# Swiglu block of a four-part float32 model on one core: gate and up products by seven block products, the down product behind all of them, the S5 table steps in new places

## Chip, core and metric

The kernel runs on one core of one Trainium2 chip, in float32 throughout. The metric is the device time of one execution in microseconds; the median of three runs before the change is 1338.49 us (1334.94 to 1342.81).

## What is computed

Two blocks over 256 tokens of width 1024. The first has two layers: a gated delta rule mixer and a swiglu, then an S5 mixer (a diagonal state space model, rewritten as convolution tables) and a mixture of eight swiglu experts. The second has pooling and neighbourhood attention and a squared-relu MLP. The change is in the swiglu of the first layer and in the S5 parameter work that is done beside it:

```python
D_FF = 11 * D_MODEL // 4                       # 2816
def swiglu(x, w1, w3, w2):
    return (jax.nn.silu(x @ w1) * (x @ w3)) @ w2
x = layer_norm(ALPHA * x + h, ln_g[i, 0], ln_b[i, 0])
f = swiglu(x, ffn_w1[j], ffn_w3[j], ffn_w2[j])
x = layer_norm(ALPHA * x + f, ln_g[i, 1], ln_b[i, 1])
```

## The kernel before

The program of each engine is written out by hand, and each engine runs its own in order; they meet at semaphores (`wait_ge`, `then_inc`). PE is TensorE, DVE VectorE, ACT ScalarE, POOL GpSimd, SP the engine whose queue carries nearly all loads; ACT and POOL issue some DMAs too. All tiles lie in one buffer, `arena`, by hand-kept offsets, and eight PSUM banks.

**Swiglu.** The 2816 columns of the hidden layer are 11 chunks of 256 (`FF_CHUNKS`), 22 tiles m of 128. x stands transposed in `xT` (8 k-blocks of 128 by 256 tokens). For a tile, `t_form` multiplies 8 weight blocks of w1 into the left half of bank 4 or 5, then 8 of w3 into the right half, each with 256 columns (the tokens). The chunk 0 is done in token halves (`half_form`), since the second half of x comes later from the layer norm. ACT takes silu of the left half into `hsil`, DVE multiplies it with the right half into `hT`. One chunk later `swiglu_down` adds the chunk's part of the down product into banks 0 to 3: 8 products with 512 columns. A float32 matmul stands as two MATMUL records in the trace. So products of gate and up and the down product alternate, chunk by chunk. SP loads a chunk as three DMAs of 1 MB (w1 and w3 in pieces of 1 KB, w2 in pieces of 4 KB) into three sets of tiles (`FF_SETS`).

**S5 work beside it.** `s5_step(m, half)` puts parameter transposes (`s5_transposes`), the transposes of the table W (`s5_turn`) and the kernel products (`s5_kernel`) between tiles: at m = 3 and 4, `S5_TURN_AT`, `S5_KERNEL_AT`. DVE makes angles, powers and the input table `Bb` behind tiles 3 to 5, and half of table V (`s5_v_table`, part 0) at `S5_TABLE_AT`. POOL waits for `Bb` (`bb_ready`), then makes for each of four pieces the table W (six operations of 1024 elements in a partition), two copies into `Bbd`, and its half of V (four of 1152 elements). Piece j+1 waits for the transposes of piece j (`w_tr`) and for its kernel products (`kd_done`). DVE takes the kernel products from PSUM (`s5_take_kernel`) and adds the skip term with two small operations per half (`s5_skip_blocks`, L1024 and L1027); ACT copies W back (`take_w`) and stores the kernel to DRAM (`store_kernel`). After the swiglu comes a layer norm, whose weights POOL loads when its last table is done, and the product with s5_w_in (L2149).

**The fill.** POOL stores zeros into `k_scratch` (semaphore `kz_stored`). ACT waits for them behind the silu of tile 1 and then issues one DMA that fills `slot_rows` in DRAM with zeros, 9600 KB, which the experts need much later.

**The model to follow.** The MLP of the second block already has seven block products in place of eight (`up_product`, `weight_sums`, L2455 and L1329 to L1334): each product multiplies a block or a sum of blocks of the weights with a block or a sum of blocks of x, and DVE makes the sums.

## Time and profile before

| | |
|---|---|
| median of 3 runs | 1338.49 us |
| the profiled execution: time, span | 1341.43 us, 1339.6 us |
| granted TensorE clock, mean | 0.987 |
| PE busy | 1292.6 us, 96% of the span |
| DVE, ACT, POOL busy | 38%, 16%, 13% |
| chain that ended last | PE 91%, DVE 5%, ACT 2% |

The span reaches from the first to the last instruction. The chain is followed back from the last instruction, at each step to what released it or to the instruction before it on its engine. Where PE has 91% of it, other engines count only where PE waits for them.

### The profile page before, as it was taken

How to read it: one execution, taken by the hardware profiler on the slowest of the kernel's cores; microseconds unless marked ns; L12 is line 12 of the kernel's file. 1: busy time of each engine (PE TensorE's matmuls, PEld its weight loads, DVE VectorE, ACT ScalarE, POOL GpSimd, SP SyncE). 2: the span in 40 equal slices, each digit the busy share in tenths (PEclk: the TensorE clock that was granted, in tenths of full speed). 3: DMA queues.
4: the chain of work that ended last, by engine and by line, in shares of the span. 5: the costliest groups of instructions: out<-in, count | busy, mean ns of one | idle time of the engine just before them, and what ended most of it. 6: DMA issues, size and time to landing. Idle time of an engine off the chain costs nothing.

```text
span 1339.6 us, 24413 instructions
## 1 busy us (share of the span) xinstructions
PE 1292.6 (96%) x10757; PEld 852.5 (64%) x10757; DVE 506.1 (38%) x982; ACT 220.9 (16%) x440; POOL 172.7 (13%) x132
## 2 busy tenths in 40 slices
PE   7998999999999999899999999999999979999997
PEld 6887987777777667645544444444445745999443
DVE  0645543334154545613211101110053164555555
ACT  1462223120111110512010101001011021111000
POOL 1020000306566600000200000000033000000000
PEclk9999999999999999999799999999999999999999
DMA  9434010599535267664899999999999060344530
GB/s 341 144 112 157 2 64 0 152 335 314 172 118 169 67 163 116 168 271 164 358 409 414 408 417 417 410 408 407 411 336 255 13 239 0 126 155 161 189 125 32
DMA packets 96934, 292.01 MB, mean 218 GB/s; under 512 B 5916, under 2 KB 43264, under 8 KB 84576
## 3 DMA queue, kind: packets, MB, share of 16 engines
q1 hardware_dynamic: 82288, 260.46, 53.2%
q0 software_dynamic: 4800, 14.67, 3.7%
q10 hardware_dynamic: 9776, 15.86, 3.6%
q8 instruction: 54, 0.88, 0.3%
q14 instruction: 16, 0.13, 0.0%
HBM read 274.19 MB, written 16.78 MB: 217 GB/s over the span
## 4 chain that ended last, share of the span: by engine, by line
PE 91%; DVE 5%; ACT 2%; issue 1%; DMA 0%; POOL 0%; DVEq 0%; ACTq 0%; POOLq 0%
PE bank L1788 19%; PE bank L2283 17%; PE bank L2300 9%; PE bank L2455 7%; PE bank L2493 7%; PE bank L1801 6%; PE bank L2093 5%; PE bank L2223 4%; PE bank L1760 3%; PE bank L2149 2%; PE bank L1794 2%; PE bank L1921 1%; PE bank L2172 1%; PE bank L1935 1%; PE bank L2109 1%
## 5 line engine op out<-in xcount | busy, mean ns | idle before, releaser
L1788 PE MATMUL bank<-xT,arena 128*128 128x256 f32 x1248 | 278.5, 382 | 2.2 <-ACT arena L1499 1.4
L1788 PEld LDWEIGHTS bank<-xT,arena 128*128 128x128 f32 x1248 | 236.5, 191 | 40.1 <-issue 6.1
L2283 PE MATMUL bank<-arena 128*32 128x352 f32 x3072 | 230.2, 461 | 0.7 <-DVE arena L1164 0.7
L2283 PEld LDWEIGHTS bank<-arena 128*32 128x32 f32 x3072 | 93.8, 111 | 134.4 <-issue 133.1
L2300 PE MATMUL bank<-arena 128*32 128x256 f32 x2112 | 115.4, 379 | 0.0
L2493 PE MATMUL bank<-arena 128*128 128x512 f32 x224 | 96.7, 592 | 0.7 <-DVE arena L1341 0.7
L2300 PEld LDWEIGHTS bank<-arena 128*32 128x32 f32 x2112 | 64.7, 110 | 50.3 <-issue 2.4
L1209 DVE TENSOR_TENSOR arena<-arena,bank 128x352 f32<-128x352 f32 x24 | 19.3, 804 | 204.4 <-PE bank L2283 204.4
L2493 PEld LDWEIGHTS bank<-arena 128*128 128x128 f32 x224 | 42.3, 190 | 53.6 <-issue 49.5
L2093 PE MATMUL bank<-arena 128*128 128x512 f32 x144 | 63.6, 594 | 0.0
L1034 DVE TENSOR_TENSOR arena<-arena,bank 128x256 f32<-128x256 f32 x22 | 9.2, 420 | 135.3 <-ACT arena L1583 135.3
L2455 PE MATMUL bank<-arena 128*128 128x128 f32 x512 | 58.5, 275 | 0.0
L2455 PEld LDWEIGHTS bank<-arena 128*128 128x128 f32 x512 | 57.8, 192 | 0.0
L1801 PE MATMUL bank<-arena 128*128 128x512 f32 x128 | 55.9, 593 | 0.5 <-DVE arena L1299 0.5
L1760 PE MATMUL bank<-const,arena 128*128 128x128 f32 x296 | 43.5, 284 | 11.5 <-DVE arena L1309 5.6
L2223 PE MATMUL bank<-arena 128*128 128x512 f32 x112 | 50.2, 609 | 2.6 <-issue 2.6
L1760 PEld LDWEIGHTS bank<-const,arena 128*128 128x128 f32 x296 | 35.1, 146 | 18.6 <-DVE arena L1309 5.6
L2093 PEld LDWEIGHTS bank<-arena 128*128 128x128 f32 x144 | 26.9, 190 | 30.9 <-issue 30.7
L2455 PE MATMUL bank<-xT,arena 128*128 128x128 f32 x384 | 44.5, 275 | 0.0
L2455 PEld LDWEIGHTS bank<-xT,arena 128*128 128x128 f32 x384 | 43.8, 192 | 1.0 <-issue 1.0
L1801 PEld LDWEIGHTS bank<-arena 128*128 128x128 f32 x128 | 23.9, 190 | 29.2 <-issue 28.2
L2223 PEld LDWEIGHTS bank<-arena 128*128 128x128 f32 x112 | 21.7, 195 | 29.8 <-issue 29.8
(401 smaller groups left out, 1416.3 us busy)
## 6 DMA issues: line engine op xcount, KB each, us to landing
arena<-moe_w SPq DMA_DIRECT2D x64, 1408.0 KB, 13.7
arena<-moe_w SPq DMA_DIRECT2D x24, 1536.0 KB, 15.5
arena<-ffn_w SPq DMA_DIRECT2D x33, 1024.0 KB, 10.2
arena<-gdn_w_in SPq DMA_DIRECT2D x8, 2048.0 KB, 10.9
arena<-w_up SPq DMA_DIRECT2D x8, 2048.0 KB, 9.0
arena<-w_down SPq DMA_DIRECT2D x8, 2048.0 KB, 7.7
slot_rows<-arena ACTq DMA_DIRECT2D x1, 9600.0 KB, 47.4
arena<-s_w_glu SPq DMA_DIRECT2D x4, 2048.0 KB, 11.9
```

Of the source, the lines that this page charges most:

```text
L1209: V_.tensor_tensor(mh[:, t].rearrange("p (x f) -> p f x", x=FE_T), msil[:, t].rearrange("p (f x) -> p f x", x=FE_T), banks[2 * t + 1][:, 0 ...
L1760: return nc.tensor.transpose(dst, src, const[0:k, C_ID, 0:k])
L1788: last = mm(bank[:, at:at + SEQ], w[:, k, P * m:P * m + P], x[:, k, :], start=(k == 0), stop=(k == KT - 1))
L1794: last = mm(bank[:, at + P * n:at + P * n + P], w[:, k, P * m:P * m + P], xT[:, k, P * n:P * n + P], start=(k == 0), stop=(k == KT - 1))
L1801: last = mm(bank, x[:, k0 + k, P * n:P * n + P], w[:, k], start=(k0 + k == 0), stop=(k0 + k == total - 1))
L2093: last = mm(banks[2 * n + hf][:, :], hT[:, c % 2, k, P * n:P * n + P], f2[c % FF_SETS][:, k, 512 * hf:512 * hf + 512], start=(c == 0 and k ...
L2149: last = mm(banks[s // 2][32 * q:32 * q + 32, 256 * (s % 2):256 * (s % 2) + 256], x_sub[:, k, s], w[:, 256 * q:256 * q + 256], start=(k == ...
L2223: last = mm(banks[4 * c + 2 * hf + n][:, :], hidT[:, k, P * n:P * n + P], glu[2 * hf + c][:, k], start=(i == 0), stop=(i == KT - 1))
L2283: last = mm(banks[i][32 * q:32 * q + 32, 0:EW1], xg[:, t, EK * s + kk], w[:, kk, EW1 * q:EW1 * q + EW1], start=(s == 0 and kk == 0), stop= ...
L2300: last = mm(y_bank[t][32 * q:32 * q + 32, 0:EW2], mhT[:, t, 32 * x:32 * x + 32], m2[c][:, x % 3, EW2 * q:EW2 * q + EW2], start=(x == 0), s ...
L2455: last = mm(bank[:, P * m:P * m + P], lhs[:, k, P * m:P * m + P], rhs[:, k], start=(i in (1, 2, 5) and m == k == 0), stop=(k == 3), skip_g ...
L2493: last = mm(d_bank[i][:, :], lhs[:, k], rhs[:, k], start=(d == k == 0), stop=(d == 7 and k == 1))
```

## The change

- Gate and up products of a chunk become seven products of 8 matmuls with 128 columns (`ffn_product`, names "1" to "7"): blocks are halves of k, of the chunk's 256 columns and of the tokens, and w1 and w3 go side by side. "1", "6", "7" and "4" add into one bank, "5" and "3" into another, "2" has its own. The order on PE is 1, 2 of chunks 0 and 1, then for each chunk c: 5(c), 6(c), 4(c-1), 3(c), 7(c), 1(c+1), 2(c+1), but no 1 and 2 behind chunk 0.
- The sums: four on the weights per chunk (`f_sum`, 1024 elements each, DVE; those of chunk 0 on POOL, ahead of the layer norm), four on x once (`f_s1`, ...). `f_sum` "1" of chunk c+1 waits for the load of chunk c+1; sum 4 of chunk c stands behind it.
- ACT copies products 1, 5 and 6 out of PSUM (`f_keep`), DVE adds them (c11, c12, c22), ACT takes silu, DVE multiplies (`f_gate`) into `f_tile`, which holds all 22 tiles.
- Weights of w1 and w3 have two buffers in place of three. Loads for chunk c+2 wait for product 7 and sum 4 of chunk c. The loads of chunk 1 come early, beside those of chunk 0.
- All down products stand behind chunk 10. The w2 loads go into places that come free.
- The S5 pieces of DVE stand behind chunks 2 to 8, `Bb` behind chunk 8; DVE's tables and kernels come after the last chunk, in the order table 0, kernel 0, table 1, kernel 1, table 2, table 3, kernel 2. PE's turns and kernels stand between the down chunks. ACT's stand in one loop behind its last chunk.
- The fill of `slot_rows` stands on ACT behind chunk 0.

```diff
-FF_SETS = 3
-S5_FIRST = 3
-S5_TURN_AT = (9, 13, 16, 19)
-S5_KERNEL_AT = (11, 15, 18)
-S5_TABLE_AT = (7, 10, 13, 16)
+S5_FIRST = 2
+S5_TURN_AT = (0, 3, 7)
+S5_KERNEL_AT = (2, 5)
...
+            def gate_loads(c):
+                cols = slice(FC * P * c, FC * P * (c + 1))
+                if c >= 2:
+                    sp.wait_ge(product, nth_p["7", c - 2])
+                    sp.wait_ge(first_sums, 4) if c == 2 else sp.wait_ge(t_sums, nth_t["4", c - 2])
+                load(sp, ("ffn_w1", c), 4 + c % 2, f13[c % 2][:, 0], w1[:, :, cols])
+                load(sp, ("ffn_w3", c), 4 + c % 2, f13[c % 2][:, 1], w3[:, :, cols])
...
-            out_load(0)
-            swiglu_loads(0)
+            gate_loads(0)
+            gate_loads(1)
             sp.wait_ge(kq_done, 4)
             sp.wait_ge(q_used, 1)
             out_load(1)
             sp.wait_ge(lv_p, 24)
             out_load(2)
             out_load(3)
-            sp.wait_ge(y_done, 4)
-            for c in range(1, FF_CHUNKS):
-                swiglu_loads(c)
+            sp.wait_ge(in_tile, 28)
+            out_load(0)
+            for c in range(2, FF_CHUNKS):
+                gate_loads(c)
...
+            sp.wait_ge(product, nth_p["7", last_c - 1])
+            sp.wait_ge(t_sums, nth_t["4", last_c - 1])
+            down_load(0)
+            down_load(1)
+            sp.wait_ge(product, nth_p["7", last_c])
+            sp.wait_ge(t_sums, nth_t["4", last_c])
+            down_load(2)
+            down_load(3)
+            sp.wait_ge(product, nth_p["4", last_c])
+            sp.wait_ge(mlp_v, nth_v["c22", "f", last_c])
+            down_load(4)
+            down_load(5)
+            for c in (6, 7, 8, 9, 10):
+                sp.wait_ge(down_done, (1, 2, 4, 5, 6)[c - 6])
+                down_load(c)
+                if c == 8:
+                    load(sp, ("s5_in", 0), 7, s5_in_w[0], rows(A["s5_w_in"][0], 0, 4))
+            sp.wait_ge(down_done, 8)
+            load(sp, ("s5_in", 1), 8, s5_in_w[1], rows(A["s5_w_in"][0], 4, 4))
             sp.wait_ge(kz_stored, 64)
             sp.wait_ge(xrow_loaded, 16)
+            table_loads(0)
             sp.wait_ge(down_done, FF_CHUNKS - 2)
+            table_loads(1)
+            sp.wait_ge(y_done, 8)
+            table_loads(2)
...
+            arrived(pool, ("ffn_w3", 0))
+            pool.wait_ge(in_tile, 32)
+            b11, b12, b21, b22 = f_blocks(0)
+            nc.gpsimd.tensor_tensor(f_t1, b12, b11, ALU.subtract).then_inc(first_sums, 1)
...
+                if c == S5_FIRST:
                     s5_angles()
+                    s5_multiples(range(0, 5))
+                elif c == S5_FIRST + 1:
+                    s5_multiples(range(5, 9))
+                    s5_reduced()
+                elif c == S5_FIRST + 2:
                     s5_take_c(1)
+                elif c == S5_FIRST + 4:
                     s5_powers()
+                elif c == S5_FIRST + 5:
+                    s5_ratio()
+                elif c == S5_FIRST + 6:
                     dve.wait_ge(s5_read, 3)
                     s5_input_table()
...
+            V_.tensor_tensor(f_s1, a21, a22, ALU.add).then_inc(s_sums, 1)
...
+            def f_sum(i, c):
+                b11, b12, b21, b22 = f_blocks(c)
+                if i == "1":
+                    arrived(dve, ("ffn_w3", c))
+                    dve.wait_ge(product, nth_p["5", c - 1])
+                    dve.wait_ge(first_sums, 4) if c == 1 else dve.wait_ge(t_sums, nth_t["2", c - 1])
+                    ins = V_.tensor_tensor(f_t1, b12, b11, ALU.subtract)
+                elif i == "2":
+                    dve.wait_ge(product, nth_p["6", c - 1])
+                    dve.wait_ge(t_sums, nth_t["1", c] if c == 1 else nth_t["4", c - 1])
+                    ins = V_.tensor_tensor(f_t2, b22, f_t1, ALU.subtract)
+                elif i == "3":
+                    dve.wait_ge(t_sums, nth_t["1", c])
+                    ins = V_.tensor_tensor(b12, b22, b12, ALU.subtract)
+                else:
+                    dve.wait_ge(product, nth_p["4", c - 1])
+                    dve.wait_ge(t_sums, nth_t["2", c])
+                    ins = V_.tensor_tensor(f_t4, b21, f_t2, ALU.subtract)
+                ins.then_inc(t_sums, 1)
...
+                V_.tensor_tensor(f_cb[:, :, 0], pair(banks[2 + c % 2]), f_u2, ALU.add).then_inc(mlp_v, 1)
+                dve.wait_ge(product, nth_p["7", c])
+                V_.tensor_tensor(f_cb[:, :, 1], pair(banks[c % 2]), f_p5, ALU.add).then_inc(mlp_v, 1)
...
+            f_first(0)
+            for c in range(FF_CHUNKS):
+                if c < last_c:
+                    f_sum("1", c + 1)
+                if c:
+                    f_sum("4", c)
+                if c < last_c:
+                    f_sum("2", c + 1)
+                if c:
+                    f_gate(c - 1, False)
+                f_gate(c, True)
+                if c < last_c:
+                    f_sum("3", c + 1)
+                f_others(c)
+                s5_pieces(c)
+                if c < last_c:
+                    f_first(c + 1)
+            f_gate(last_c, False)
+            for j, take in ((0, 0), (1, 1), (2, None), (3, 2)):
                 for q in range(2):
+                    p0 = PIECE * j + 4 * q
+                    s5_v_table(V_, link, slice(p0, p0 + 4), 0, t_v).then_inc(v_ready, 1)
+                    dve.wait_ge(v_ready, 2 * j + q + 1)
+                if take is not None:
+                    s5_take_kernel(take)
+                    s5_skip_blocks(take, 0)
+                    s5_skip_blocks(take, 1)
...
+            for c in range(FF_CHUNKS):
+                f_keep("5", c, banks[2 + c % 2], f_p5, "p5", ("c22", "f", c - 1) if c else None)
+                f_keep("6", c, banks[c % 2], f_u2, "u2", ("c12", "f", c - 1) if c else None)
+                if c:
+                    f_silu_others(c - 1)
+                f_silu_first(c)
+                if c < last_c:
+                    f_keep("1", c + 1, banks[(c + 1) % 2], f_p1, "p1", ("c11", "f", c))
+                if c == S5_FIRST - 2:
                     act.wait_ge(kz_stored, 64)
...
+            f_silu_others(last_c)
+            for j in range(NPIECE):
+                take_w(j, 0)
+                take_w(j, 1)
+                if j < NPIECE - 1:
+                    store_kernel(j)
...
+                if i == "1":
+                    arrived(pe, ("ffn_w3", c))
+                    if c >= 2:
+                        pe.wait_ge(mlp_a, nth_a["c21", "f", c - 2])
+                    lhs, rhs = b11, a11
+                elif i == "2":
+                    if c >= 2:
+                        pe.wait_ge(mlp_v, nth_v["c11", "f", c - 2])
+                    lhs, rhs = b21, a12
+                elif i == "5":
+                    if c >= 2:
+                        pe.wait_ge(mlp_v, nth_v["c12", "f", c - 2])
+                    summed(1)
+                    pe.wait_ge(s_sums, 1)
+                    lhs, rhs = f_t1, f_s1
+                elif i == "6":
+                    pe.wait_ge(mlp_a, nth_a["p1", "f", c])
+                    summed(2)
+                    pe.wait_ge(s_sums, 2)
+                    lhs, rhs = f_t2, f_s2
+                elif i == "3":
+                    pe.wait_ge(mlp_a, nth_a["p5", "f", c])
+                    pe.wait_ge(s_sums, 4)
+                    lhs, rhs = b22, f_s4
+                elif i == "7":
+                    pe.wait_ge(mlp_a, nth_a["u2", "f", c])
+                    summed(3)
+                    lhs, rhs = b12, a21
+                else:
+                    pe.wait_ge(mlp_v, nth_v["c22", "f", c])
+                    summed(4)
+                    lhs, rhs = f_t4, a22
+                for w in range(2):
+                    for k in range(4):
+                        last = mm(bank[:, P * w:P * w + P], lhs[:, w, k], rhs[:, k], start=(i in ("1", "2", "5") and w == k == 0),
+                                  stop=(k == 3), skip_group_check=True)
+                last.then_inc(product, 1)
...
+            ffn_product("1", 0)
+            ffn_product("2", 0)
+            ffn_product("1", 1)
+            turn_x(xres, 1, 0)
+            ffn_product("2", 1)
+            need_x()
+            for c in range(FF_CHUNKS):
+                ffn_product("5", c)
+                ffn_product("6", c)
+                if c:
+                    ffn_product("4", c - 1)
+                if c == S5_FIRST:
+                    s5_transposes(0)
+                ffn_product("3", c)
+                ffn_product("7", c)
+                if c == S5_FIRST:
+                    s5_transposes(1)
+                if c == S5_FIRST + 1:
                     s5_transposes(2)
+                if 1 <= c < last_c:
+                    ffn_product("1", c + 1)
+                    ffn_product("2", c + 1)
+            down_ready(0)
...
+            for c in range(FF_CHUNKS - 2):
+                if c:
+                    down_ready(c)
+                for n, hf in ((0, 0), (0, 1), (1, 0), (1, 1)) if c else ((1, 0), (0, 0)):
+                    if c == 0:
+                        pe.wait_ge(mlp_v, nth_v["c12", "f", last_c]) if n else pe.wait_ge(mlp_a, nth_a["c21", "f", last_c])
+                    if (n, hf) == (1, 0) and c in S5_TURN_AT:
+                        s5_turn(S5_TURN_AT.index(c), 0)
+                    if (n, hf) == (1, 0) and c in S5_KERNEL_AT:
+                        s5_kernel(S5_KERNEL_AT.index(c), 0)
+                    last = down_part(c, n, hf)
...
+            for i in range(2):
+                s5_kernel(2, i)
+            down_ready(last_c - 1)
+            down_ready(last_c)
+            for n, hf in ((0, 0), (0, 1), (1, 0), (1, 1)):
+                down_part(last_c - 1, n, hf)
+                if n and hf:
+                    turn_x(xres, 0, 2)
+                down_part(last_c, n, hf).then_inc(y_done, 1)
+                if n != hf:
+                    s5_turn(3, n)
```

## Rows read from the trace of the kernel before

**Rows 1.** The page, section 4: the chain by engine.
```profile
PE 91%; DVE 5%; ACT 2%; issue 1%; DMA 0%; POOL 0%; DVEq 0%; ACTq 0%; POOLq 0%
```

**Rows 2.** Windows, whole swiglu stage: length, busy by engine, clock, DMA share, GB/s.
```profile
250.20:493.80 243.60, 243.60 (x1157) 181.40 (x1157) 97.23 (x191) 31.16 (x53) 118.07 (x71) 1.00 0.61 201
```

**Rows 3.** The chain in order of time: start, duration, what.
```profile
250.18 5.36 PE bank L1794 x48
...
256.41 8.93 PE bank L1794 x80
...
310.68 13.81 PE bank L1788 x64
324.49 6.87 PE bank L2093 x16
...
501.79 17.93 PE bank L2149 x326
...
1140.72 92.96 PE bank L2455 x832
```

**Rows 4.** DVE's groups by form, 1140.7 to 1233.7: busy, mean ns, idle before.
```profile
L1329 DVE TENSOR_TENSOR arena<-arena 128x1024 f32<-128x1024 f32 x7 | 8.6, 1225 | 8.3 <-PE bank L2455 8.3
...
L1380 DVE TENSOR_TENSOR arena<-bank,arena 128x256 f32<-128x256 f32 x8 | 3.4, 424 | 5.2 <-PE bank L2455 5.2
...
L1339 DVE TENSOR_TENSOR arena<-xT 128x512 f32<-128x512 f32 x1 | 0.7, 692 | 0.0
```

**Rows 5.** Timeline of ACT, around its wait for the zero stores.
```profile
277.46 0.41 ACTq L1586 DMA_DIRECT2D slot_rows<-arena  x1
277.97 0.48 ACT L1583 ACTIVATE arena<-bank,small 128x256 f32<-128x256 f32 x1 [12.12 <-DMA k_scratch<-arena]
```

**Rows 6.** Timeline of POOL: the zero stores, the first table operation.
```profile
268.05 2.31 POOL L454 DMA_DIRECT2D k_scratch<-arena  x4 [0.29 <-POOL arena L452]
...
313.20 2.02 POOL L403 TENSOR_TENSOR arena<-arena 128x1024 f32<-128x1024 f32 x1 [42.31 <-DVE arena L405]
```

**Rows 7.** DMA issues: size of each, median us to landing (ffn_w: 350 to 400).
```profile
arena<-ffn_w SPq DMA_DIRECT2D x9, 1024.0 KB, 7.8
...
slot_rows<-arena ACTq DMA_DIRECT2D x1, 9600.0 KB, 47.4
...
k_scratch<-arena POOLq DMA_DIRECT2D x4, 128.0 KB, 6.6
```

**Rows 8.** Queues (q10 ACT's, q1 SP's): 277.5 to 282, then 284 to 308.
```profile
q10 hardware_dynamic: 51, 0.21, 12.1%
...
q10 hardware_dynamic: 1586, 6.50, 76.7%
q1 hardware_dynamic: 1585, 2.36, 26.1%
```

**Rows 9.** Windows, at the end of a pause of PE (idle until 119.5).
```profile
118.00:124.00 6.00, 4.48 (x23) 4.46 (x24) 5.90 (x13) 0.00 (x0) 0.00 (x0) 0.72 1.10 364
```

**Rows 10.** Windows, POOL's tables: columns as in Rows 2, POOL's busy time is fifth.
```profile
313.20:463.20 150.00, 150.00 (x701) 110.85 (x700) 62.29 (x74) 15.13 (x30) 101.56 (x48) 1.00 0.46 151
```

**Rows 11.** Timeline of DVE: POOL idle at 407, busy from 429.48.
```profile
407.08 0.76 DVE L404 TENSOR_TENSOR norm_w<-arena 128x576 f32<-128x576 f32 x1
...
430.12 2.47 DVE L404 TENSOR_TENSOR norm_w<-arena 128x576 f32<-128x576 f32 x1
432.62 2.46 DVE L405 TENSOR_TENSOR arena<-arena,norm_w 128x576 f32<-128x576 f32 x1
435.12 2.25 DVE L1024 TENSOR_TENSOR arena<-const,small 32x64 f32<-32x64 f32 x1
...
439.40 0.40 DVE L1034 TENSOR_TENSOR arena<-arena,bank 128x256 f32<-128x256 f32 x1
```

**Rows 12.** Timeline of POOL at the same time.
```profile
429.48 2.49 POOL L403 TENSOR_TENSOR arena<-arena 128x1024 f32<-128x1024 f32 x1 [4.28 <-PE bank L1760]
432.05 2.42 POOL L404 TENSOR_TENSOR norm_w<-arena 128x1024 f32<-128x1024 f32 x1
```

More of the change, by code:

```diff
@@ L114, in build, with pair @@
         banks = [ctx.enter_context(nc.psum_tensor(f"bank{i}", [P, 512], F32)) for i in range(8)]
+        def pair(bank):
+            return bank[:, 0:2 * P].rearrange("p (a b) -> p a b", a=2)
         def region(off, *dims, parts=P):
@@ L382, in arrived, with f_blocks @@
             eng.wait_ge(*arrival[key])
+        def f_blocks(c):
+            u = f13[c % 2]
+            return (u[:, :, 4 * k:4 * k + 4, P * f:P * f + P] for k in range(2) for f in range(2))
         def after(eng, sem_, value):
@@ L943, in s5_angles, with s5_multiples @@
                 link(V_.tensor_tensor(z, lam, dts[:, None, :].broadcast_to((P, 2, PAIRS)), ALU.mult))
-                for k in range(9):
+            def s5_multiples(ks):
+                for k in ks:
                     V_.tensor_scalar(pw_mag[:, k], z[:, 0], float(k), None, ALU.mult)
@@ L949, in s5_angles, with s5_reduced @@
                 link(last)
+            def s5_reduced():
                 ROUND = 12582912.0
@@ new lines, in down_part, with down_ready @@
+            def down_part(c, n, hf):
+                for k in range(FC):
+                    last = mm(banks[2 * n + hf][:, :], f_tile(2 * c + k, n), f2[c][:, k, 512 * hf:512 * hf + 512],
+                              start=(c == 0 and k == 0), stop=(c == last_c and k == FC - 1))
+                return last
+            def down_ready(c):
+                arrived(pe, ("ffn_w2", c))
+                pe.wait_ge(mlp_v, nth_v["h21", "f", c])
+            ffn_product("1", 0)
+            ffn_product("2", 0)
```

261 lines of the change are left out of this document (127 added, 134 removed).

## Prediction

> **What bounds the kernel now.** I read the page's chain first: PE holds 91% of it [rows 1], so a stage is worth what its matrix work costs, unless it gets waits. The window over the swiglu stage shows that now it has none: PE is busy 243.60 of 243.60 us, while DVE works 97, POOL 118 and the DMA engines move 201 GB/s, of some 370 that they reach when full [rows 2, 8]. The pieces of the chain give the prices [rows 3]: a chunk's gate and up products are 64 matmul records of 256 columns in 13.81 us, its down product 16 records of 512 columns in 6.87 us. Inside the stage I then looked for engines that are late without hurting. ACT waits 12.12 us for the zero stores into k_scratch and only then issues the fill of slot_rows, at 277.46 [rows 5]; POOL begins its S5 tables at 313.20 [rows 6] and ends them at 463.2, busy for 101.56 us of 150 [rows 10].
>
> **The matrix work.** The second block already runs seven products with 128 columns: 832 records in 92.96 us, 0.1117 us each [rows 3]. A chunk of the change has 7 x 16 = 112 of them, 12.51 us; one product is 1.79. Before: ten chunks of 13.81 and chunk 0 in halves, 128 x 0.1117 = 14.3, together 152.4. After: 11 x 12.51 = 137.6. The gain is **14.8 us**. The 88 down matmul pairs (11 x 6.87), the S5 transposes and kernels and the x transposes are as many as before. The input sums of 512 elements take 0.69 us [rows 4]; PE ends the x transposes at 256.41 [rows 3], the copy takes as long, and the first sum is ready at about 257.9, before PE has done product 2 of chunk 1 (256.41 + 1.79 = 258.2): nothing.
>
> **DVE's sums.** Four sums of 1024 elements per chunk at 1.225 us, three PSUM additions at 0.42 [rows 4], three gate products at 0.2 to 0.4: about 7 us per chunk, and at most 5 more for a piece of S5 work, inside 12.5. Alone, DVE is hidden. The loads of chunk c+2 go out when product 7 of c ends, and two loads of 1 MB land 7.8 us after issue [rows 7], I take 9 for the pair with a margin; they are wanted after 12.5. Hidden too, as long as nothing else uses the queues.
>
> **First wait: the fill.** ACT's program is in order. After chunk 0 it waits for kz_stored, then issues the fill, and only then takes product 5 of chunk 1, without which PE can't start product 3 of chunk 1. Before, PE had two more half chunks to do meanwhile. Now, from 258.2, PE has four products of chunk 0 and three (5, 6, and 4 of chunk 0) until 270.7. The zero stores are issued by POOL from 268.05 to 270.4 [rows 6] and took 6.6 us to land [rows 7], beside 6 MB of SP's loads that are no longer there; I put their end at 274 (bounds 272.4 and 277.5). PE waits about 4 us; product 7 of chunk 1 ends at 278.5, and chunk 2, whose loads went out at 265.4, has landed by then.
>
> The loads of chunk 3 need product 7 of chunk 1 and sum 4 of chunk 1, which DVE makes behind sum 1 of chunk 2, so they go out at 280.6 and move from 282.6. The fill's packets begin some 4 us after its issue, as before (51 of them by 282 [rows 8]), so at 278. Both use the same 16 DMA engines. While they run together the trace counts 1586 packets of the fill (6.50 MB) and 1585 of SP (2.36 MB) in 24 us [rows 8]: one for one, 66 per us each. A weight packet is 1 KB, a fill packet 4 KB. Chunk 3's 2 MB are 2048 packets: 31 us, until 313.6; the fill has 9600 KB, 2400 packets, and landed after 47.4 us [rows 7], with a thin last part, which would be 321 now. As the load is spread over the engines like the fill, I take **318** (bounds 312 and 323). PE has finished chunk 2 at 291 and stands idle for 27 us. DVE stands in sum 1 of chunk 3, so the loads of chunk 4 go out only after it, at 320, land at 329, before PE is through with chunk 3. After a pause of PE that ended at 119.5 the granted clock was 0.72 over 6 us [rows 9], 1.7 us of work lost; the same here. Product 7 of chunk 3 ends at 318 + 12.5 + 1.7 = 332.2. Without waits it would be 258.2 + 7.1 + 8.9 + 25.0 = 299.3: **+32.9 us**. Bounds: 4 (only the wait for the zero stores) and 38.
>
> **Second wait: DVE beside POOL, in chunks 9 and 10.** POOL's S5 tables need Bb, which DVE now makes in chunk 8. Product 7 of chunk 8 ends at 332.2 + 5 x 12.5 = 394.7, Bb is ready at 402. Then POOL's ops of 2 to 3 us meet DVE's two-input ops in SBUF. Alone a 576-element op takes 0.76 us; beside POOL it took 2.47 and 2.46, and a 32x64 op 2.25 [rows 11]: each ends half a microsecond after a POOL op ends [rows 12]. An op with one operand in PSUM took 0.40 at the same time [rows 11]. So a DVE op on SBUF costs a POOL op, some 2.45 us if it is short and 3.3 if it has 1024 elements. In chunk 9 DVE has seven of them (sums 1, 4, 2, three gates, sum 3) from 403.7 on, 20 us, before it adds the blocks c12 and c22; PE wants c22 for product 4 of chunk 9 at 414.4 and gets it at 424. In chunk 10 four more hold product 4 by 3 us. PE ends product 4 of chunk 10 at 437.8 in place of 424.9: **+12.9 us** (bounds 0, if DVE slipped in between, and 18, if each of the eleven costs a long op of 3.1).
>
> **Third wait: the S5 chain in the down product.** Before, it had the whole stage; now POOL starts at 402 and three pieces of 101.56 / 4 = 25.4 us [rows 10] and DVE's tables lie in the 76 us of the down product. DVE has 24 two-input table ops and 12 small ones (L1024, L1027), nearly all beside POOL. Walk: kernel 0 at 457; DVE's four small ops behind POOL's last four of piece 1 to 469; its six table ops behind POOL's next six to 481.5, where PE wants kernel 1 at 475; table 2 until 505, table 3 until 520, the small ops of piece 2 until 531.5. ACT's take_w of piece 3 stands behind store_kernel(2), so PE's last transposes wait for the same op, and the layer norm on DVE, which could have read its first bank at 513, begins at 531.5. xT is complete at 548. Without this wait it would be 501.8 [rows 3] - 14.8 + 32.9 + 12.9 = 532.8: **+15.4 us** (bounds 0 and 25). The norm weights, which POOL loads after its last table, land at about 536 and are no later than the rest.
>
> The Trainium skill (SBUF — State Buffer, section "Who interferes with whom") says that a DVE instruction with two SBUF inputs and a GpSimd one that reads SBUF exclude each other for a whole instruction. In the rows one in three or four slips by at 0.75 us, which the sum allows for; by the rule taken strictly some four more would wait, and the time would be about 1393.
>
> **Elsewhere.** Four sums on POOL at 216 lie in its idle time before the norm. The w2 loads (4 KB packets, 1 MB each) are issued one to two chunks of 6.87 us ahead; s5_w_in comes earlier than before; table loads 0 and 1 too, and table 2 with 16 issues after the last down product has 50 us until it is read. All nothing.
>
> **Sum.** The profiled execution has a span of 1339.6 and a time of 1341.43, 2.9 above the runs' median. 1339.6 - 14.8 + 32.9 + 12.9 + 15.4 = 1386.0 of span, 1387.8 of time, 1385 as a median.
>
> **Rivals.**
> (a) The fill does no harm: SP's packets get through, or they land before it starts. For it: chunk 2's loads were ahead of it, and PE did not stop before. Against it: rows 8, and chunk 3 can't be asked for before 280. It leaves 4 to 5 of 32.9: about 1357. Chance 0.12.
> (b) DVE and POOL pass each other, or the S5 chain has slack enough: second and third wait gone, about 1357. For it: the ops on PSUM are free, and before PE never waited. Against: rows 11 and 12, and DVE's order puts the block additions behind the sums. Chance 0.18.
> (c) Faster: the matrix work sets the end, as now. One mechanism: PE has other products ready wherever an engine is late, because each wait is three products ahead of its use. Place: the 11 chunks; price -14.8, so 1324. It decides while all waits together stay under 8 us. For it: PE 243.60 of 243.60 [rows 2] in spite of ACT's 12 us. Against: with two buffers PE has one chunk of 12.5 us ahead, and the fill holds a load for 30. Chance 0.09; waits of 8 to 21 us, no change, 0.03.
> (d) Still slower: DVE late in every piece, above 1402: 0.06.
> The forecast itself, 1366 to 1402, has 0.52.
>
> **Numbers.** What a measurement can tell here is 0.5%, 6.7 us. Slower: 0.52 + 0.12 + 0.18 + 0.06 = 0.88; within 0.5% 0.03; faster 0.09. The range must take in (a) and (b) with their spread of some 10 us, and ends where the forecast ends: 1346 to 1402.
>
> **What would show it.** PE: a gap of about 4 us in chunk 1 that ends with ACT's copy after the fill; one of 20 to 30 us ahead of chunk 3 that ends with a DMA of ffn_w, the clock low behind it; one of some 9 us in chunk 9 that ends with DVE's addition. The load of chunk 3 takes over 30 us to land. DVE's sums take 1.22 us until chunk 8 and 2 to 3.5 then. Products: 1.79 us each. Last table op of POOL near 530, the layer norm behind the small ops L1024/L1027's successors. I am wrong if chunk 3's load lands before 300, or if PE stays busy in chunks 9 and 10.

## The result and the profile after

The changed kernel takes 1388.78 us (median of 4 runs, 1387.79 to 1391.95), the kernel before 1338.25 beside it (4 runs, 1334.94 to 1342.81): ratio 1.0386, with a 95% interval of 1.0369 to 1.0404. The forecast was 1385, range 1346 to 1402. The profiled execution has a span of 1390.1 us and a time of 1391.95.

The page's chain by engine after, against PE's 91% before [rows 1]:

```profile
PE 81%; DVE 7%; DMA 5%; POOL 3%; issue 2%; ACT 2%; SPq 0%; ACTq 0%; DVEq 0%; POOLq 0%
```

The page's two groups of the seven products (busy, mean ns of one, idle before and what ended it):

```profile
L2293 PE MATMUL bank<-xT,arena 128*128 128x128 f32 x704 | 87.8, 285 | 31.6 <-DMA arena<-ffn_w 25.0
L2293 PE MATMUL bank<-arena 128*128 128x128 f32 x528 | 64.4, 280 | 6.4 <-ACT arena L1728 6.4
```

DMA and POOL, both at 0% before, have entered the chain, and DVE has 7% where it had 5%. What PE waited for inside the stage (view of the waits, PE, 245 to 560 us: total, times, longest):

```profile
PE bank L2293 <- DMA arena<-ffn_w: 25.0, 1, 25.0
PE bank L1934 <- ACT arena L1721: 8.4, 2, 4.5
PE bank L2293 <- DVE arena L1159: 6.6, 2, 4.7
PE bank L2293 <- ACT arena L1728: 6.4, 1, 6.4
PE bank L1934 <- DVE xres L957: 3.2, 2, 2.8
PE bank L1934 <- DVE arena L1080: 2.9, 2, 2.4
```

Windows of the stage (length, busy PE, PEld, DVE, ACT, POOL, PEclk, DMA share, GB/s), where before PE was busy throughout at a clock of 1.00 [rows 2]:

```profile
279.00:319.00 40.00, 15.06 (x141) 14.54 (x139) 1.75 (x4) 5.22 (x10) 0.00 (x0) 0.75 0.78 251
319.00:334.00 15.00, 14.92 (x119) 14.80 (x120) 12.90 (x38) 2.35 (x7) 0.00 (x0) 0.88 0.45 141
334.00:397.00 63.00, 63.00 (x569) 62.83 (x568) 44.47 (x108) 15.92 (x41) 0.00 (x0) 1.00 0.53 168
397.00:438.00 41.00, 34.40 (x259) 31.95 (x258) 32.82 (x31) 5.58 (x17) 28.39 (x12) 0.92 0.44 154
438.00:552.00 114.00, 98.72 (x391) 47.73 (x392) 80.09 (x86) 11.91 (x22) 77.06 (x40) 0.92 0.52 139
```

There is a hole of 25 us without POOL, five chunks that run as meant, then a stretch where PE loses time whenever POOL works. The chain in order of time names both:

```profile
265.95 6.53 DMA k_scratch<-arena
272.50 0.40 ACTq L1757
273.43 6.08 PE bank L2293 x32
279.93 39.11 DMA arena<-ffn_w
319.08 14.39 PE bank L2293 x112
334.98 62.74 PE bank L2293 x560
398.15 7.87 DMA arena<-ffn_w
407.32 3.05 DVE arena L1140
410.46 3.19 DVE arena L1133
434.37 3.11 PE bank L2293 x16
```

The same form of load takes 39.11 us behind the fill and 7.87 later. 560 records in 62.74 us are five chunks of 12.55, as the second block's price said [rows 3]. DVE's sums (L1140, L1133) take two and a half times the 1.2 us of [rows 4] as soon as POOL has begun. The piece of 7.87 us ahead of them is the load of chunk 10: DVE stood 1.4 us for it with its first sum, a delay that the forecast didn't have. What POOL does at the end of the down product (timeline, last piece), and DVE beside it:

```profile
505.39 2.09 POOL L432 TENSOR_TENSOR arena<-arena 128x1024 f32<-128x1024 f32 x1 [4.26 <-PE bank L1934]
529.40 3.12 POOL L456 TENSOR_SCALAR arena<-arena 128x1152 f32<-128x1152 f32 x1
532.82 0.62 POOL L678 DMA_DIRECT2D norm_w<-ln_g  x1 [0.30 <-POOL arena L456]
```

```profile
504.84 0.76 DVE L434 TENSOR_TENSOR arena<-arena,norm_w 128x576 f32<-128x576 f32 x1
505.64 2.46 DVE L432 TENSOR_TENSOR arena<-arena 128x576 f32<-128x576 f32 x1
508.13 2.46 DVE L433 TENSOR_TENSOR norm_w<-arena 128x576 f32<-128x576 f32 x1
529.42 2.94 DVE L1092 TENSOR_TENSOR arena<-arena 32x64 f32<-32x64 f32 x1
538.26 1.41 DVE L952 SCALAR_TENSOR_TENSOR xres<-xres,small,norm_w 128x512 f32<-128x512 f32 x2 [2.76 <-DMA norm_w<-ln_b]
```

The same DVE operation takes 0.76 us before POOL starts at 505.39 and 2.46 after. DVE begins the layer norm of the stage's end at 532.39, right behind its last small operation (L1092), and stands in it once more, 2.76 us, for the norm weights, which POOL asks for after its last table. The input product of S5, at 501.79 before [rows 3], begins at 551.50; from there on the two kernels are equal (837.8 and 838.6 us).

For the experiments I cut the stage in two: from PE's first gate product to the end of its last one (product 4 of chunk 10), and from there to S5's input product. After: 191.3 (246.2 to 437.5) and 114.0 us, in all 305.3, against 251.6 before (250.18 to 501.79). These lengths come from one profile each. The starts of the stage differ by up to 4.7 us between them, which is why lengths are compared and not ends; and early_fill and early_late, which differ only behind the first half, have first halves of 159.6 and 161.9, so a difference of 2 us between two profiles says nothing.

### The profile page after: what moved, and what is told of

Same layout as the page of the kernel before. It is cut to its first block, busy times and chain, and to the rows that moved or that the text cites. A ratio compares the mean times of both kernels' runs of the same rounds, so it can differ in the third digit from the quotient of the medians.

```text
span 1390.1 us, 25612 instructions
## 1 busy us (share of the span) xinstructions
PE 1291.0 (93%) x11221; PEld 861.8 (62%) x11221; DVE 591.8 (43%) x1070; ACT 234.5 (17%) x494; POOL 183.5 (13%) x136
## 4 chain that ended last, share of the span: by engine, by line
PE 81%; DVE 7%; DMA 5%; POOL 3%; issue 2%; ACT 2%; SPq 0%; ACTq 0%; DVEq 0%; POOLq 0%
PE bank L2512 16%; PE bank L2529 8%; PE bank L1962 8%; PE bank L2684 7%; PE bank L2722 7%; PE bank L2293 6%; PE bank L1975 6%; PE bank L2452 4%; PE bank L2300 4%; DMA arena<-ffn_w 3%; PE bank L1934 3%; PE bank L2378 2%; PE bank L2095 1%; PE bank L2109 1%; PE bank L2401 1%
## 5 line engine op out<-in xcount | busy, mean ns | idle before, releaser
L1962 PE MATMUL bank<-xT,arena 128*128 128x256 f32 x608 | 134.1, 380 | 2.3 <-ACT arena L1645 1.3
L1962 PEld LDWEIGHTS bank<-xT,arena 128*128 128x128 f32 x608 | 114.3, 190 | 18.9 <-ACT arena L1645 1.8
L2293 PE MATMUL bank<-xT,arena 128*128 128x128 f32 x704 | 87.8, 285 | 31.6 <-DMA arena<-ffn_w 25.0
L2293 PEld LDWEIGHTS bank<-xT,arena 128*128 128x128 f32 x704 | 85.3, 201 | 33.5 <-DMA arena<-ffn_w 25.3
L2722 PE MATMUL bank<-arena 128*128 128x512 f32 x224 | 96.7, 592 | 0.7 <-DVE arena L1487 0.7
L2300 PE MATMUL bank<-arena 128*128 128x512 f32 x176 | 84.2, 630 | 0.0
L2722 PEld LDWEIGHTS bank<-arena 128*128 128x128 f32 x224 | 42.3, 190 | 53.6 <-issue 49.5
L2293 PE MATMUL bank<-arena 128*128 128x128 f32 x528 | 64.4, 280 | 6.4 <-ACT arena L1728 6.4
L2293 PEld LDWEIGHTS bank<-arena 128*128 128x128 f32 x528 | 62.3, 196 | 6.7 <-ACT arena L1728 6.6
L2300 PEld LDWEIGHTS bank<-arena 128*128 128x128 f32 x176 | 34.7, 205 | 39.0 <-issue 39.0
L1975 PE MATMUL bank<-arena 128*128 128x512 f32 x128 | 58.1, 612 | 0.5 <-DVE arena L1445 0.5
L2684 PE MATMUL bank<-arena 128*128 128x128 f32 x512 | 58.5, 275 | 0.0
L2684 PEld LDWEIGHTS bank<-arena 128*128 128x128 f32 x512 | 57.8, 192 | 0.0
L2452 PE MATMUL bank<-arena 128*128 128x512 f32 x112 | 50.2, 610 | 2.7 <-issue 2.7
L432 POOL TENSOR_TENSOR arena<-arena 128x1024 f32<-128x1024 f32 (+1 forms) x12 | 27.1, 2254 | 155.0 <-DVE arena L434 137.2
## 6 DMA issues: line engine op xcount, KB each, us to landing
slot_rows<-arena ACTq DMA_DIRECT2D x1, 9600.0 KB, 45.5
```

What stands on the lines that cost most here:

```text
L432: link(eng_ns.tensor_tensor(dst, pa, qa, ALU.mult))
L1962: last = mm(bank[:, at:at + SEQ], w[:, k, P * m:P * m + P], x[:, k, :], start=(k == 0), stop=(k == KT - 1))
L1975: last = mm(bank, x[:, k0 + k, P * n:P * n + P], w[:, k], start=(k0 + k == 0), stop=(k0 + k == total - 1))
L2293: last = mm(bank[:, P * w:P * w + P], lhs[:, w, k], rhs[:, k], start=(i in ("1", "2", "5") and w == k == 0), stop=(k == 3), skip_group_che ...
L2300: last = mm(banks[2 * n + hf][:, :], f_tile(2 * c + k, n), f2[c][:, k, 512 * hf:512 * hf + 512], start=(c == 0 and k == 0), stop=(c == las ...
L2452: last = mm(banks[4 * c + 2 * hf + n][:, :], hidT[:, k, P * n:P * n + P], glu[2 * hf + c][:, k], start=(i == 0), stop=(i == KT - 1))
```

## The experiments

The runs come from several chips, and each was timed beside the kernel before. The third column is the median less that of the kernel before beside it; it is the one to compare between rows.

| run | median, us | above the kernel before beside it, us | first half, us | second half, us |
|---|---|---|---|---|
| changed kernel | 1388.78 | 50.5 | 191.3 | 114.0 |
| fill_1k | 1381.59 | 42.1 | 179.9 | 115.1 |
| v_on_dve | 1385.76 | 46.2 | 188.9 | 109.4 |
| early_fill | 1357.91 | 18.4 | 159.6 | 113.7 |
| early_late | 1358.41 | 21.0 | 161.9 | 114.6 |
| early_vdve_late | 1354.30 | 16.9 | 158.5 | 109.9 |
| early_pool_late | 1362.84 | 25.5 | 150.9 | 122.7 |
| no_pool_tables | not comparable | | 150.9 | 95.3 |
| all_dve | 1337.98 | 0.2 | 150.7 | 101.3 |
| all_dve_tuned | 1331.79 | -6.2 | 152.2 | 93.2 |

**early_fill.** The fill of slot_rows moves into the delta rule's recurrence, from a zero row of its own. That row lies where `f_tile` 8 is written later, so DVE waits for the end of the fill ahead of chunk 4's gate (`dve.wait_ge(xrow_loaded, 16)`, not shown in the cut below).

```diff
+            pool.wait_ge(in_tile, 28)
+            nc.gpsimd.memset(zrow, 0.0).then_inc(zrow_ready, 1)
...
             take_z(28)
+            act.wait_ge(zrow_ready, 1)
+            act.dma_start(slots.rearrange("a s d -> s a d"), zrow[:, None, :].broadcast_to(...)).then_inc(xrow_loaded, 16)
...
-                if c == S5_FIRST - 2:
-                    act.wait_ge(kz_stored, 64)
-                    act.dma_start(slots.rearrange("a s d -> s a d"), ...)
```

> The changed kernel with one thing moved: ScalarE issues the fill of the expert slots with zeros after it has taken tile 28 of the input projection, inside the delta rule's recurrence, from a row of zeros of its own that GpSimd sets there, in place of between the gates of chunks 0 and 1. My theory (the fill holds chunk 3's weights up: their load took 39.1 us against some 7, TensorE stood 25.0 us for it and ScalarE 6.4 us for the zero stores ahead of the fill, and the clock had to be won back for 1.9 us): the 25 us wait and the 6.4 us wait both go, time 1357 (1353 to 1361), ratio to the changed kernel 0.977. Rival 1 (chunk 3's load is slow by itself, since chunks 2 and 3 are asked for together after the recurrence and the fill only fills gaps): time stays within 5 us of 1389. Rival 2 (it is only taken from one place to another, the fill now holding up something in the recurrence): a wait on a load of the output weights or of chunk 0 or 1 before 250 us and 1365 to 1389.

Measured: 1357.91 us (4 runs; ratio to the kernel before 1.0145, 1.0104 to 1.0185): 18.4 above the kernel before where the changed kernel is 50.5 above, so 32.1 less. First half 159.6, second 113.7: the stage is 32.0 shorter, nearly all of it in the first half. The waits for ACT's copy and the 25 us are gone; one of 3.3 us for chunk 2's weights is left. Both rivals fall: the fill took 41.4 us in the recurrence and held nothing there.

**before_early_fill.** The same move in the kernel before. Here SP too waits for the end of the fill, ahead of the loads of chunk 1.

> The kernel before with the same move of the fill. My theory: its fill and the same length of loads collide there too, but three sets of weights were in place before it, so that TensorE never waited for them: within 3 us of 1338. Rival (the fill costs about as much there, hidden in the products' lower rate, and moving it is simply good): 1325 or less.

Measured: 1339.08, ratio 0.9994 (0.9980 to 1.0008). The fill cost nothing there; its price comes with the change. The likely reason is that the change has two sets of gate weights where there were three, but no run gives the changed kernel a third set, so this is argued and not shown.

**fill_1k.** The fill at its place in the changed kernel, cut finer.

```diff
-  act.dma_start(slots.rearrange("a s d -> s a d"), kzero[0:SLOTS, None, :].broadcast_to((SLOTS, MAX_PASS * EXPERTS + 1, DM)))
+  act.dma_start(slots.rearrange("a s d -> (a s d)").rearrange("(s r d) -> s r d", s=SLOTS, d=256),
+                kzero[0:SLOTS, None, 0:256].broadcast_to((SLOTS, 4 * (MAX_PASS * EXPERTS + 1), 256)))
```

> The changed kernel with the same fill at the same place, of the same 9600 KB, cut into pieces of 1 KB in place of 4 KB. If the two queues are served one packet each in turn, whatever its size, the share of chunk 3's weights rises from a quarter or less of the bytes to a half: the load of chunk 3 lands 12 to 18 us after its issue (39.1 before), TensorE's wait for it falls from 25.0 to 4 or less, the time is 1364 to 1372. Rival (the bytes of both queues are what counts, shared in some other way, or all of the first queue's packets are served ahead): load and wait stay above 30 and 18 us and the time is 1384 or more. A third case: the small pieces make the fill so much slower in bytes that it also reaches into the loads of chunks 4 and 5; then its landing is above 60 us and the time between.

Measured: 1381.59 (1.0318, 1.0295 to 1.0342), 42.1 above the kernel before in place of 50.5, so 8.4 less; the stage is 10.3 shorter. The chain has two loads in place of one, and the queues (q10 the fill, q1 the weights: packets, MB, share) for 284 to 303 us read:

```profile
282.48 20.84 DMA arena<-ffn_w
306.19 18.09 DMA arena<-ffn_w
```

```profile
q10 hardware_dynamic: 4074, 4.17, 72.9%
q1 hardware_dynamic: 2080, 2.10, 31.2%
```

The weights of chunk 3 land in 20.8 us in place of 39.1, so the size of the other queue's packets matters, as the step on the fill had it. Over these 19 us there are two packets of the fill to one of the weights, but this window takes in the start and the tail of the load: its packets begin some 4 us after its issue, and only 42 of them are left for the window's last microsecond. Where both queues are in full flow, from 290 to 298 us, they are served one for one, in this run:

```profile
q10 hardware_dynamic: 1396, 1.43, 58.7%
q1 hardware_dynamic: 1343, 1.36, 47.9%
```

and in the changed kernel, whose fill has pieces of 4 KB:

```profile
q10 hardware_dynamic: 526, 2.15, 83.0%
q1 hardware_dynamic: 525, 0.53, 18.8%
```

The rule of sharing in my theory holds; its price does not. I had put the load at 12 to 18 us, without its start and tail, and had not counted that the fill, which now lands after 48.4 us (45.5 in the changed kernel), still runs when chunk 4 is asked for: the second load takes 18.1 us and PE's two waits are 11.0. From 284 to 303 us both kernels move 331 GB/s: the bytes that the fill doesn't take from one load it takes from the next.

**v_on_dve.** DVE makes POOL's half of table V too.

```diff
-                s5_v_table(nc.gpsimd, link, pr, 1, t_p).then_inc(im_ready, 1)
...
+                    link(s5_v_table(V_, link, slice(p0, p0 + 4), 1, t_v))
                     s5_v_table(V_, link, slice(p0, p0 + 4), 0, t_v).then_inc(v_ready, 1)
```

> The changed kernel with the second half of table V (GpSimd's three products of 1152 values and one scaling, 10.2 us a piece with the gaps) made by VectorE, in halves of 4 pairs beside the half that it makes already. My theory (GpSimd's chain sets the end of the down product: 26 us of work in each of the last pieces of 31, with its last table at 532.5): GpSimd's share of a piece falls to 16 us, its last operation comes by 517, the input product of S5 starts 10 to 17 us earlier against the start of the gate products, and in chunk 10 the waits of TensorE on VectorE's sums lose some 2 to 4 us: time 1374 (1369 to 1380). Rival 1 (VectorE's take and add of the kernel's blocks, ScalarE's store behind them and the next transposes behind that store set each piece, not GpSimd): the piece keeps its 31 us, time 1384 to 1390. Rival 2 (VectorE with 4 more operations of 0.76 to 2.5 us on each half becomes the bound): time above 1390.

Measured: 1385.76 (1.0341, 1.0318 to 1.0365), 46.2 above the kernel before, so 4.3 less; halves 188.9 and 109.4, together 7.0 shorter. My theory that POOL's work alone sets the end falls. POOL is freed and stands still instead (its timeline, the table of the last piece), while PE waits 7.3 us in two places for DVE's table, 6.7 of it ahead of kernel 0:

```profile
508.60 2.22 POOL L432 TENSOR_TENSOR arena<-arena 128x1024 f32<-128x1024 f32 x1 [14.81 <-PE bank L1937]
```

**early_late.** On top of early_fill, ACT stores a piece's kernel after the next piece's copies.

```diff
                 take_w(j, 1)
-                if j < NPIECE - 1:
-                    store_kernel(j)
+                if j:
+                    store_kernel(j - 1)
```

> The kernel with the early fill, and ScalarE's store of a piece's kernel blocks put behind its copies of the next piece's transposes (in place of ahead of them). With the early fill alone TensorE still stood 8.9 us in two places for these copies, the longest 4.5 us, in the down product, while ScalarE stood 27 us at a time for VectorE's sums ahead of a store. My theory (each piece of the S5 tables is held by the chain block sums on VectorE, store on ScalarE, copy of the transposes, next transposes, next table on GpSimd): both waits go, GpSimd's waits for transposes (15.5 us, 3 times) fall under 9, its last table and the norm's weights land 5 to 9 us earlier; time 1350 (1346 to 1354). Rival (GpSimd's own work of 26 us a piece sets the pace, the copies only hit what had slack): the two waits turn into a later wait of TensorE on the layer norm, time 1355 to 1360.

Measured: 1358.41 (1.0155, 1.0138 to 1.0172), 21.0 above the kernel before where early_fill is 18.4 above, no gain; halves 161.9 and 114.6. The two waits for ACT's copies are gone, and PE waits for others (its waits, whole stage):

```profile
PE bank L1939 <- DVE xres L961: 9.0, 2, 8.6
PE bank L2298 <- DVE arena L1163: 6.6, 2, 4.8
PE bank L2251 <- DVE arena L436: 5.8, 1, 5.8
```

This is nearly the rival's case. POOL starts piece 2 without a wait at 442.95, in the midst of DVE's V table, and DVE's five operations behind it take 2.46 to 2.79 each, where the same operations take 0.76 beside an idle POOL. What one engine gains by starting earlier the other pays.

**early_vdve_late.** The last two edits together, with the early fill.

> The early fill, the late store, and the second half of table V on VectorE in place of GpSimd. Alone this last move won some 3 us, since TensorE's transposes then held GpSimd. My theory (two coupled limits: GpSimd's work a piece and the store ahead of the copies; each hides the other): together with the late store GpSimd's last table comes 8 us or more before that of the late store alone, time 1344 (1338 to 1350). Rival (VectorE's eight more operations a piece, at 2.5 us beside GpSimd, now hold the kernel blocks and with them the end): 1350 or more, with TensorE waiting for VectorE's table in the down product.

Measured: 1354.30 (1.0121, 1.0103 to 1.0138); halves 158.5 and 109.9. That is 4.1 less than the late store alone, and PE waits 7.3 us for DVE's tables: the rival's case. I had thought of two limits that hide each other; three edits that each free one engine have now given 4 us, nothing and 4 us.

**early_pool_late.** With the early fill, POOL's tables begin after product 7 of chunk 10.

```diff
             pool.wait_ge(bb_ready, 1)
+            pool.wait_ge(product, nth_p["7", last_c])
```

> The kernel with the early fill, and GpSimd's first table put off until the last gate product of chunk 10 is made, some 27 us later. My theory (both prices of the forecast hold: VectorE's sums beside GpSimd cost TensorE some waits in chunk 10, and GpSimd's chain sets the end of the down product): TensorE's waits for VectorE's sums before the down product (5.0 us, and 0.91 of the clock behind them) go, VectorE's sums stay at 1.22 us, and the end of the chain moves later by 15 to 22 us: time 1370 (1364 to 1377). Rival 1 (the end is not GpSimd's): the time falls by the 5 to 7 us of the waits, to 1351. Rival 2 (the sums beside GpSimd cost nothing on the path, TensorE would wait there anyway): the waits before the down product stay.

Measured: 1362.84 (1.0186, 1.0150 to 1.0223), below my range; its interval overlaps that of early_fill, so the two times can't be told apart, and the stage is as long as there (273.6 and 273.3). Its parts differ. The first half falls by 8.7 us, which is what DVE beside POOL costs the gate products (in early_fill waits of 5.0 us and PE at a clock of 0.91 from 367 to 407 us). The second grows by 9.0 and not by 15 to 22: POOL begins 18 us later and not 27, and its four tables now run without a pause, from 392.10 to 500.61, 27.1 us a piece, where they had stood 9.9 us for PE's first transposes.

**no_pool_tables.** With the early fill, POOL's tables left out.

```diff
-                    s5_w_table(nc.gpsimd, link, j, part, t_p).then_inc(w_ready, 1)
+                    nc.gpsimd.memset(Wp[:, part, :, :, 0:1], 0.0).then_inc(w_ready, 1)
...
-                s5_v_table(nc.gpsimd, link, pr, 1, t_p).then_inc(im_ready, 1)
+                nc.gpsimd.memset(V[:, 1, pr, :, 0:1], 0.0).then_inc(im_ready, 1)
```

> The early fill, and GpSimd's tables left out (of each product and sum a small memset in their place, so that the S5 layer is not computed as it should be); VectorE's half of V stays. What TensorE waits for is then not GpSimd. My theory (without GpSimd's tables nothing but TensorE's own work sets the stage, some 7 us in chunk 10 and 12 to 16 us at its end are GpSimd's, directly and by VectorE's slowed operations): the waits for VectorE's sums go, VectorE's operations of 576 values take 0.76 us throughout, time 1335 (1330 to 1340). Rival (the order of the transposes, the layer norm behind the last products and the clock cost the same without it): 1348 or more.

Measured: 1688.46, a time that can't be compared, since what comes after the stage works on other values and is longer; the stage can. Its halves are 150.9 and 95.3, together 27.1 less than in early_fill, where I had expected some 23 of the time (1335 against 1357.91). POOL's tables, with what they do to DVE, thus cost the stage 8.7 us in the first half (as in early_pool_late) and 18.4 in the second. DVE's 576-element operations take 0.76 us throughout.

**all_dve.** If two engines shut each other out, one of them should do it all. DVE makes W and V, piece by piece; POOL copies. Three more things differ from early_fill, of which the cut below shows one: the transposes of the first two pieces come a chunk later, ACT stores late as in early_late, and the norm weights are asked for as soon as the last W is made.

```diff
-S5_TURN_AT = (0, 3, 7)
+S5_TURN_AT = (1, 4, 7)
...
+            for j in range(NPIECE):
+                if j:
+                    dve.wait_ge(w_tr, 4 * j)
+                for part in range(2):
+                    s5_w_table(V_, link, j, part, t_p).then_inc(w_ready, 1)
+                    dve.wait_ge(w_ready, 2 * j + part + 1)
+                if j:
+                    s5_take_kernel(j - 1)
...
+                    s5_v_table(V_, link, pr, 1, t_p).then_inc(v_ready, 1)
+                    dve.wait_ge(v_ready, 2 * j + 1)
+                    s5_v_table(V_, link, pr, 0, t_p).then_inc(v_ready, 1)
```

> The early fill and the late store, and all tables of S5 (W and both halves of V) made by VectorE after its last gate, piece by piece (W, take of the last piece's kernel, V), GpSimd keeping only its copies; the transposes of the first two pieces one chunk later, the norm's weights asked for as soon as the last W is made (the last V uses another scratch). My theory (both engines are held in turn by operations with two operands from SBUF: GpSimd's 1024 values take 2.0 us alone and hold VectorE up 1.7 us each, while VectorE would make the same table itself in 1.2 to 1.35; so GpSimd's 108 us of tables cost more than they relieve): VectorE needs 17 to 18 us a piece for tables and 3 for blocks, and reaches the layer norm some 80 us after its last gate; TensorE's waits for the sums in chunk 10 (5.0 us) go, and the input product of S5 starts 20 to 25 us earlier against the early fill alone: time 1335 (1329 to 1342). Rival (VectorE as the only maker becomes the bound, its chain longer than the down product by 10 us or more, TensorE waiting for a V table or a take): 1345 or more.

Measured: 1337.98 (11 runs; 1.0004, 0.9991 to 1.0017), 18.2 less than with the early fill alone when each is taken against the kernel before beside it. Halves 150.7 and 101.3, together 21.3 shorter. No run parts the gain of the tables from that of the earlier norm weights; in the changed kernel these held the layer norm for 2.76 us, and the late store alone had gained nothing. A table of 1024 elements takes DVE 1.23 us an operation, one of 1152 1.36; POOL took 2.0 to 2.8 and held DVE for 1.7 of it. A piece with its blocks takes DVE some 20 us (W(1) at 416.61, W(2) at 437.27), less than the 27.1 that POOL took for its share alone.

**all_dve_tuned.** The order is fitted to that kernel's own waits. The cut shows it against all_dve; the call of `s5_kernel(2, ...)` behind the last products goes with the new entry of `S5_KERNEL_AT`.

```diff
-S5_TURN_AT = (1, 4, 7)
-S5_KERNEL_AT = (2, 5)
+S5_TURN_AT = (1, 4, 6)
+S5_KERNEL_AT = (2, 5, 7)
...
+                if c == last_c:
+                    s5_w_table(V_, link, 0, 0, t_p).then_inc(w_ready, 1)
                 dve.wait_ge(mlp_a, nth_a["c21", "f", c])
```

> The kernel with the early fill, the late store and all tables on VectorE, laid out anew by its own trace, in which VectorE stood 4.1 us for the transposes of piece 2, 4.4 us ahead of its last gate, and TensorE 1.5 us for the first W table and 5.9 us for the layer norm behind VectorE's last table: the first half of table W(0) is made ahead of the last gate, the transposes of piece 2 and the kernel products of piece 2 come one chunk earlier. My theory (VectorE's chain is the last limit of the stage): VectorE comes to the layer norm 8 us earlier after the last gate product, TensorE's two waits fall from 7.4 to 2 us or less, time 1332 (1328 to 1335), 0.3 to 0.7% under the kernel before. Rival (the last products and the layer norm behind them hold the input product anyway): no gain over 1338.

Measured: 1331.79 (9 runs), ratio 0.9946 (0.9927 to 0.9966): 0.5% faster than the kernel before, a small gain, but the interval leaves 1 out, and the stage is shorter by the same 6.2 us. Halves 152.2 and 93.2. PE's waits of the stage, all of them, and the windows of its down products:

```profile
PE bank L2311 <- DMA arena<-ffn_w: 3.4, 1, 3.4
PE bank L1952 <- DVE xres L959: 2.1, 2, 1.7
PE bank L2394 <- DVE xT L776: 0.8, 1, 0.8
PE bank L1952 <- issue: 0.8, 1, 0.8
```

```profile
404.00:440.00 36.00, 36.00 (x144) 17.38 (x146) 32.55 (x36) 4.30 (x8) 1.48 (x2) 1.00 0.56 213
440.00:475.00 35.00, 35.00 (x151) 16.32 (x144) 33.63 (x52) 2.15 (x4) 4.29 (x6) 1.00 0.50 146
```

PE is full again beside a DVE that is busy for 66 of 71 us; POOL, at 77.06 of 114 us after, works 5.8.

## Why the forecast held, step by step

**The matrix work, -14.8.** Right: 12.55 us a chunk against 12.51. It is there and is seen once the waits are gone: the tuned kernel's stage is 245.4 us against 251.6 before. Of the 8.6 us that are still missing (251.6 - 14.8 would be 236.8), 3.4 are the wait for chunk 2's weights and some 3 the clock (0.94 over the first 55 us); the rest I put down to the layer norm, where PE waits 2.1.

**The fill, +32.9.** Right in each link. The zero stores ended at 272.48 (forecast 274, with everything 3.8 us early), PE waited 6.4 us for ACT's copy (4), the load of chunk 3 landed at 319.04 (318) and PE stood 25.0 us for it (27); the chunk behind the pause took 14.39 us for 12.51, 1.9 of clock (1.7). early_fill puts the sum at 32.1 by the times and 32.0 by the stage. The step's picture of two queues served packet for packet held too: 525 of the weights to 526 of the fill over 8 us here, 1343 to 1396 with equal packets in fill_1k.

**DVE beside POOL in chunks 9 and 10, +12.9.** Right in place and kind, too large in size: 8.7 us by the first halves of early_fill and early_pool_late, known to some 2 us. PE waited twice, ahead of product 4 of chunk 9 (4.7 us, forecast 9.6) and of product 4 of chunk 10 (1.9, forecast 3). The sums took what was forecast (3.05 and 3.19 us), but not all seven operations of chunk 9 were held: in the trace of early_fill, sum 1 took 1.28 us and a gate 0.28. Against that, DVE's first sum stood 1.4 us for its load in the trace after, where the step had put nothing.

**The S5 chain in the down product, +15.4.** Right in size, and right in most of its links: 18.4 us (113.7 in early_fill against the 95.3 of no_pool_tables). DVE began the layer norm at 532.39 behind its last small operation (forecast 531.5), and PE's last transposes waited 3.9 us for ACT's copy behind the store that the same operation releases, as said. Two things were wrong. The norm weights, called no later than the rest, landed at 538.16 and not at 536 and held the layer norm for 2.76 us, behind POOL's own 27.1 us for its last piece (25.4 by [rows 10]). And the wait that I had put ahead of kernel 1 did not come: PE waited 4.5 us at the transposes of piece 1 instead, also for ACT's copy behind a store.

**The sum, and the luck in it.** The three terms were 61.2 together and measure 59.1 (the stage of 305.3 against the 246.2 of no_pool_tables). Missing from my sum were 9.4 us that stay when fill and POOL's tables are both gone (246.2 where 251.6 - 14.8 = 236.8 was due): the parts named above under the matrix work. The start of the stage, some 4 us earlier in this profile than in the one before, hid nearly half of them. So the forecast of 1385 for 1388.78 is nearer than its working: 9.4 us were left out, and against them stood 2.1 too much in the terms and the early start, which is chance. I can't tell where the early start comes from: it arises ahead of the stage, and in the profiles of the experiments, whose code is the same there but for the fill, the stage starts anywhere from 246.1 to 250.7.

**The rule of exclusion.** The Trainium skill (SBUF — State Buffer, section "Who interferes with whom") has a DVE instruction with two SBUF inputs and a GpSimd one that reads SBUF exclude each other for the whole instruction. The traces after agree: 0.76 us before 505.39 and 2.46 behind it, 3.05 for 1.2, with few exceptions, which run in a gap between two operations of POOL. From these numbers follows what all_dve used: as long as DVE has such work waiting, an operation on POOL costs it 1.7 us (2.46 - 0.76), more than its own making of the same 1024 elements (1.23).

## What to carry to other kernels

When matrix work is cut, look first at what it covered: here the gain of 14.8 us was real, but the kernel before had covered a fill of 9600 KB, most likely by its third set of weights, and its longer stage had covered the tables of the next layer. A large transfer that nothing waits for belongs where no load is near, and in front of double buffers it is paid for: here 32 us for a fill that took 45. Two elementwise engines that lock each other are one engine: count their two-input operations together, and if the faster one can do the slower one's share in the time it is held, give it all.

## What the hardware showed that I had not expected

- Freeing one of the two locked engines gave 4.3 us, nothing and 4.1 us, handing all table work to one 18.2 (with the norm weights asked for earlier).
- Cutting the fill's packets from 4 KB to 1 KB, with its bytes and the total rate (331 GB/s from 284 to 303 us) unchanged, let the competing load land in 20.8 us in place of 39.1: the queues were served packet for packet at either size.
- A DVE operation of 32x64 elements, 0.2 us alone, took 2.2 to 2.9 us beside POOL (but for one of 0.77), as much as one of 576 columns (2.46). From 404 to 535 us of the trace after, the twelve small ones, nearly all beside POOL, took 28.9 us (13.2 and 15.7), and the 24 of the tables, many of them beside an idle POOL, 30.7.
